# Modulation's matrix-vector product moved from the first FFN to the branch merge, and waits per tile in place of four barriers

## The chip, the cores and the metric

The kernel runs on one core of one Trainium2 chip. The metric is the time of one execution on the device in microseconds (us), the median of three runs. A core has TensorE (PE, matmuls), VectorE (DVE), ScalarE (ACT), GpSimd (POOL) and SyncE (SP), which here only issues DMAs. Each engine runs its own instructions in order and waits on semaphores for the others.

## The reference

The program is three transformer blocks one after the other on 512 tokens of width 1024, all in float32. The two places that matter here are the merge of the first block's two branches, and the modulation of the third block, which depends on nothing but two inputs:

```python
# first block
g_a, g_b = jnp.split(gates, 2, axis=-1)
mixed = jax.nn.sigmoid(g_a) * ya + jax.nn.sigmoid(g_b) * yb
x = x + mixed @ w_out[l]
h = rmsnorm(x, norm_ffn_g[l])
u = causal_dwconv(h @ w_up[l], ffn_conv_w[l], ffn_conv_b[l])
val, gt = jnp.split(u, 2, axis=-1)
x = x + (jax.nn.gelu(gt) * val) @ w_down[l]
...
# third block
mod = (jax.nn.silu(c) @ w_ada[l] + b_ada[l]).reshape(b_, N_SUB, 3, D_MODEL)
shift, scale, gate = mod[:, :, 0], mod[:, :, 1], mod[:, :, 2]
```

w_ada is 1024 x 9216, c one row of 1024: a matrix-vector product that reads 36 MB. ya and yb are the outputs of the two branches, each a product of its own.

## The kernel before

Activations lie feature-major: tiles k = 0 to 7 of 128 features by 512 tokens. X is the residual; HH and HL are the high and low parts of the normalised input, YH and YL those of another operand. Every matmul of float32 precision is three matmuls of reduced precision (`exact3`, L312): high by high, high by low, low by high. A tile of 128 output features over 8 k is 24 matmuls.

Weights come in 189 panels of 128 x 2048 (1 MB), two tiles of the usual kind each, through two slots. For each panel SP issues the DMA into WT (`panel`, L223), ACT casts it into WH (`next_panel`, or `hi` in the FFN loops), POOL subtracts into WL (`low`, L275), and PE opens it (`open_panel`) once POOL is done. SP may load a panel when POOL has finished the one two before it (w_lo), ACT may cast it when PE has opened the one before (w_used). G_MERGE, G_OUT1 and G_FFN1 are panels 15, 27 and 31.

The order is written out by hand in blocks of code, one per engine. Around the change it is: the diff attention branch (da); the merge, four times two gate panels and one branch panel, in which ACT takes sigmoids of the gates into GS and DVE multiplies and adds into MIX; OUT1, four panels, with DVE adding the result to X (`add_out`, L1650); FFN1, eleven chunks of two up panels and one down panel; a small embedding stage, stick-breaking attention (SB), OUT2, latent attention (MLA), OUT3, FFN2, the third block's mixer with OUT4, and FFN3. `end_phase` is a barrier of PE, ACT and DVE: each drains, counts up phase_end and waits for the two others.

The first tiles of an FFN are "raw": PE works on the input before it is normalised, and DVE scales the result in the accumulator (by NRS, L1891), while `normalise` makes HH and HL for the others.

The modulation is 36 slabs of w_ada (1 MB each, three buffers ADA), in halves: DVE multiplies a half-slab by the row CROW, silu(c) (`ada`, L1868), ACT sums it over its 1024 columns into a column of MOD (`sums`, L1226). SP issues them in FFN1's loop, three panels then three slabs a chunk (L259); a slab waits for the sums of the slab three before (ada_used).

## Time and profile before

| | |
|---|---|
| median of 3 runs | 2812.05 us (2810.21 to 2819.77) |
| profiled execution | 2812.49 us, span 2810.7 us, TensorE's mean granted clock 0.945 |
| busy share of the span | PE 89%, PE weight load 71%, DVE 49%, ACT 36%, POOL 37% |
| merge, 367.7 to 500.4 | 132.7 us, PE 132.65 busy |
| OUT1, 510.7 to 556.5 | 45.8 us, PE 45.78 busy |
| DMA | 245.49 MB, mean 87 GB/s |

A row of a timeline has the start, the length, the engine with the line of the kernel, the operation with its output and inputs, and in brackets how long the engine sat idle before it and who released it. Matmuls overlap: their spacing from start to start is shorter than their length. The clock of TensorE is given as a share of full speed (2.4 GHz); 0.5 is its lower level. A q behind an engine's name (SPq, DVEq) means its instruction queue. The landing of a DMA is counted from its issue.

### The profile page before, as it was taken

To read this page: it belongs to the slowest core of one execution; us is meant where nothing else is said; L and a number is where in the kernel's file an instruction comes from. 1 tells how busy PE (TensorE), PEld (TensorE's weight loads), DVE (VectorE), ACT (ScalarE), POOL (GpSimd) and SP (SyncE) were. 2 spreads that over 40 slices of the span, in tenths; PEclk is the share of its full clock that TensorE was granted. 3 is DMA by queue.
4 is the path that set the end of the run, shared out by engine and by line. 5 is a ranking of instruction groups with operands and counts; after the bars stand their busy time and mean duration, and the time that the engine had idled before them with its cause. 6 is when DMAs were issued, how large, how long until landed. Compare 5 with 4: busy or idle time off the path is not lost.

```text
span 2810.7 us, 31316 instructions
## 1 busy us (share of the span) xinstructions
PE 2515.1 (89%) x11582; PEld 1998.7 (71%) x11582; DVE 1377.8 (49%) x1881; ACT 1018.1 (36%) x1294; POOL 1034.5 (37%) x758
## 2 busy tenths in 40 slices
PE   7968889879999789998898889999979998899996
PEld 5636668657777668776776677888858766588885
DVE  6373621478888865244444554232265343622225
ACT  4322422333334453466436533122234332322211
POOL 3202134435555344222343234445434203254442
PEclk9878999989999999999898999999989998899998
DMA  3102012324444322111122112222312101122221
GB/s 139 50 30 75 31 60 105 135 105 179 179 182 189 152 76 90 61 45 46 60 90 75 46 53 83 91 103 90 104 60 85 69 17 60 45 90 104 90 101 48
DMA packets 35811, 245.49 MB, mean 87 GB/s; under 512 B 3935, under 2 KB 3935, under 8 KB 7044
## 3 DMA queue, kind: packets, MB, share of 16 engines
q1 hardware_dynamic: 34704, 241.73, 23.8%
q10 hardware_dynamic: 1012, 2.45, 0.3%
q8 instruction: 65, 1.06, 0.1%
q14 instruction: 30, 0.25, 0.0%
HBM read 242.06 MB, written 2.11 MB: 87 GB/s over the span
## 4 chain that ended last, share of the span: by engine, by line
issue 57%; POOL 27%; PE 13%; DVE 2%; DVEq 0%; POOLq 0%; ACT 0%; ACTq 0%
POOL WL L279 27%; PE PS L314 4%; PE PS L315 4%; PE PS L316 4%; DVE X L2186 0%; DVE ARENA L2181 0%; DVE ARENA L1591 0%; DVE ARENA L1609 0%; POOLq L283 0%; DVEq L2185 0%; DVE ARENA L1616 0%; DVE ARENA L2313 0%; DVEq L1632 0%; PE PS L372 0%; POOLq L276 0%
## 5 line engine op out<-in xcount | busy, mean ns | idle before, releaser
L279 POOL TENSOR_TENSOR WL<-WT,WH 128x512 fp32r<-128x512 f32 x754 | 1034.3, 1403 | 1734.6 <-ACT WH L960 1225.9
L314 PE MATMUL PS<-HH,WH 128*128 128x512 f32 x1520 | 609.6, 401 | 47.4 <-DVE HL L1623 12.8
L316 PE MATMUL PS<-HH,WL 128*128 128x512 f32 x1520 | 599.9, 395 | 0.0
L315 PE MATMUL PS<-HL,WH 128*128 128x512 f32 x1520 | 599.6, 395 | 0.0
L314 PE MATMUL PS<-YH,WH 128*128 128x512 f32 x904 | 363.6, 402 | 59.2 <-ACT ARENA L954 18.9
L314 PEld LDWEIGHTS PS<-HH,WH 128*128 128x128 f32 x1520 | 290.5, 191 | 126.9 <-issue 26.5
L1238 ACT CAST WH<-WT 128x2048 fp32r<-128x2048 f32 x90 | 172.1, 1912 | 559.9 <-PE PS L314 559.9
L315 PE MATMUL PS<-YL,WH 128*128 128x512 f32 x904 | 358.3, 396 | 0.0
L316 PE MATMUL PS<-YH,WL 128*128 128x512 f32 x904 | 358.0, 396 | 0.0
L316 PEld LDWEIGHTS PS<-HH,WL 128*128 128x128 f32 x1520 | 290.0, 191 | 62.4
L315 PEld LDWEIGHTS PS<-HL,WH 128*128 128x128 f32 x1520 | 290.8, 191 | 58.0 <-issue 0.9
L960 ACT CAST WH<-WT 128x2048 fp32r<-128x2048 f32 (+1 forms) x99 | 187.4, 1893 | 199.3 <-PE PS L314 156.9
L954 ACT ACTIVATE ARENA<-PS 128x512 f32<-128x512 f32 (+1 forms) x162 | 111.5, 693 | 396.6 <-PE PS L316 286.9
L314 PEld LDWEIGHTS PS<-YH,WH 128*128 128x128 f32 x904 | 173.0, 191 | 108.6 <-ACT ARENA L954 20.0
L954 ACT ACTIVATE ARENA<-ARENA 128x512 f32<-128x512 f32 (+6 forms) x195 | 167.4, 878 | 165.8 <-DVE ARENA L1763 44.4
L1905 DVE TENSOR_TENSOR ARENA<-PS,ARENA 128x512 f32<-128x512 f32 x44 | 30.4, 692 | 376.6 <-PE PS L316 376.6
L316 PEld LDWEIGHTS PS<-YH,WL 128*128 128x128 f32 x904 | 173.5, 192 | 37.6
L315 PEld LDWEIGHTS PS<-YL,WH 128*128 128x128 f32 x904 | 173.8, 192 | 34.7
L1927 DVE TENSOR_TENSOR ARENA<-PS,ARENA 128x512 f32<-128x512 f32 x176 | 121.7, 691 | 114.9 <-PE PS L316 113.4
L389 PE MATMUL PS<-HH,WH 128*128 128x512 f32 x256 | 110.4, 431 | 41.2 <-DVE HL L1603 19.9
L954 ACT ACTIVATE ARENA<-PS,COLS 128x128 f32<-128x128 f32 (+3 forms) x102 | 57.7, 567 | 190.4 <-DVE COLS L2264 72.5
L314 PE MATMUL PS<-WH,HH 128*128 128x256 f32 x384 | 112.3, 292 | 14.5 <-DVEq L1573 7.2
(285 smaller groups left out, 3387.2 us busy)
## 6 DMA issues: line engine op xcount, KB each, us to landing
WT<-weights SPq DMA_DIRECT2D x188, 1024.0 KB, 4.8
ARENA<-w_ada SPq DMA_DIRECT2D x36, 1024.0 KB, 6.7
X<-x_fm SPq DMA_DIRECT2D x4, 512.0 KB, 8.0
out_fm<-X SPq DMA_DIRECT2D x8, 256.0 KB, 2.0
ARENA<-rel_rows ACTq DMA_DIRECT2D x1, 1024.0 KB, 5.2
CON<-constants SPq DMA_DIRECT2D x1, 704.0 KB, 10.1
WT<-weights SPq DMA_DIRECT2D x1, 512.0 KB, 5.4
ARENA<-rows SPq DMA_DIRECT2D x1, 512.0 KB, 5.8
```

The costliest lines, as they stand in the source:

```text
L279: i = nc.gpsimd.tensor_tensor(WL[s][:, e], WT[s][:, e], WH[s][:, e].bitcast(F32), ALU.subtract)
L314: i0 = nc.tensor.matmul(o, w[0], r[0], start=first, stop=False, skip_group_check=True)
L315: nc.tensor.matmul(o, w[0], r[1], start=False, stop=False, skip_group_check=True)
L316: i2 = nc.tensor.matmul(o, w[1], r[0], start=False, stop=last, skip_group_check=True)
L389: i0 = nc.tensor.matmul(psb(b), w[0], src[0][:, k, :], start=k == 0, stop=False, skip_group_check=True)
L954: return nc.scalar.activation(o, i, fn, **kw)
L960: nc.scalar.copy(WH[s][:, 0:width], WT[s][:, 0:width]).then_inc(sem("w_hi"), 1)
L1238: nc.scalar.copy(WH[s][:, :], WT[s][:, :]).then_inc(sem("w_hi"), 1)
L1905: free(tt(GT[:, q, :], psb(b), GE[:, q, :], ALU.mult), b)
L1927: tt(dst[:, j, :], psb(4 + j % 4), dst[:, j, :], ALU.add).then_inc(sem("b_read"), 1)
```

## The change

The modulation's 72 half-slabs move from FFN1 to the merge (60) and OUT1 (12). The row silu(c) lies in accumulator banks 4 and 5 (CROWP) instead of in SBUF. The four barriers after the diff attention, after the merge, before OUT2 and before OUT3 go; the branch panels wait for da_done, and an output GEMM's first tile waits for each of its eight input tiles (mix_ready, sy_ready, mly_ready). MIX is split into HH and HL tile by tile in DVE's last merge step. The raw input of FFN1 goes to YH and YL, so that four tiles of chunk 0 can be raw. In all FFNs the last chunk's product is made during the down GEMM of the chunk before it (`early`), the last two chunks standing outside the loop. Three norm sums add their last square on PE instead of DVE (`two_parts`), and PE waits for the constants at the first norm sum instead of before the first tile.

```diff
         a = Carve()
         CV, GE, GT = a.tiles(4), a.tiles(2), a.tiles(2)
         ada_at = a.at
+        a = Carve(ada_at + 3 * 2048)
+        PIN = a.tiles(2)
+        a = Carve(14 * S)
         ADA = [a(2048) for _ in range(3)]
-        PIN = a.tiles(2)
         CROW = a(D)
+        CROWP = PSF[:, 4 * S:4 * S + D]
         ACC = ARENA[:, ada_at:ada_at + DT * S].rearrange("p (k n) -> p k n", k=DT)
 
         a = Carve()
...
-            stream(2, G_FFN1 + 2)
-            sp.wait_ge(sem("phase_end"), 3 * 3)
+            stream(2, G_MERGE + 2)
+            sp.wait_ge(sem("da_done"), 1)
             sp.dma_start(CROW, rows_in[:, 1536:1536 + D]).then_inc(sem("c_dma"), 16)
-            sp.dma_start(PIN, p_in).then_inc(sem("p_dma"), 16)
             for k in range(3):
                 ada(k, k, first=True)
-
-            with sp.Fori(0, (CH - 1) // 2) as i:
-                for h in range(2):
-                    g = G_FFN1 + 2 + 6 * i + 3 * h
-                    for k in range(3):
-                        panel(g + k, (G_FFN1 + 3 * h + k) % 2)
-                    for k in range(3):
-                        ada(3 + 6 * i + 3 * h + k, k)
-            panel(G_FFN1 + 3 * CH - 1, (G_FFN1 + 3 * CH - 1) % 2)
+            for i in range(12):
+                panel(G_MERGE + 2 + i, (G_MERGE + 2 + i) % 2)
+                for k in range(3 if i < 10 else 0):
+                    ada(3 + 3 * i + k, k)
+            stream(G_MERGE + 14, G_FFN1)
             for k in range(3):
-                ada(NADA - 3 + k, k)
-            stream(G_PLE, n_panels)
+                ada(33 + k, k)
+            stream(G_FFN1, G_FFN1 + 2)
+            sp.wait_ge(sem("ada_used"), NADA)
+            sp.dma_start(PIN, p_in).then_inc(sem("p_dma"), 16)
+            stream(G_FFN1 + 2, n_panels)
             store()
 
 
...
-            def out_gemm(g0):
+            def out_gemm(g0, src, ready):
                 for g in range(g0, g0 + 4):
                     open_panel(g)
-                    feature_tiles(g, g % 2, 8, 256, y_hi, y_lo, (0, P))
+                    for c in (0, P):
+                        b = take()
+                        for k in range(DT):
+                            if g == g0 and c == 0:
+                                pe.wait_ge(sem(ready), k + 1)
+                            i0, i2 = exact3(psb(b), wtile(g % 2, 8, 256, k, c, c + P), (src[0][:, k, :], src[1][:, k, :]), k == 0, k == DT - 1)
+                            if c == 0 and k == 0:
+                                used(g, i0)
+                        i2.then_inc(sem("a_done"), 1)
...
-            end_phase()
 
 
             for jp in range(4):
                 for q in range(2):
                     panel_h(G_MERGE + 3 * jp + q)
                 g = open_panel(G_MERGE + 3 * jp + 2)
+                pe.wait_ge(sem("da_done"), 1)
                 ym = lambda k, o=0: YH[:, k + o, :]
                 for j in range(2):
                     for br in range(2):
                         feature_tiles(g, g % 2, 4, 256, lambda k: YH[:, 4 * br + k, :], lambda k: YL[:, 4 * br + k, :],
                                       (P * j,), base=1024 * br, first_of_panel=(j == 0 and br == 0))
-            pe.wait_ge(sem("mix_ready"), 1)
-            end_phase()
-            out_gemm(G_OUT1)
-
-
-            def ffn(g0, sums="one", shift=None):
+            out_gemm(G_OUT1, (HH, HL), "mix_ready")
...
-                        if raw and q < 2:
-                            raw_tile(g, P * q, b, opens=q == 0, sums=None if q else sums, last=q == 1,
+                        if raw and q < raws:
+                            raw_tile(g, P * (q % 2), b, src, opens=q % 2 == 0, sums=None if q else sums, last=src[0] is HH and q == raws - 1,
                                      shift=None if shift is None else (shift, SHIFT_BANKS[q]))
-                            if q:
+                            if q == raws - 1:
...
-                            i0, i2 = exact3(psb(b), wtile(s, 2, D, k, P * j, P * j + P), (YH[:, k, :], YL[:, k, :]), k == 0, k == 1)
+                            i0, i2 = exact3(psb(b), wtile(s, 2, D, k, P * j, P * j + P), (YH[:, 4 * last + k, :], YL[:, 4 * last + k, :]), k == 0, k == 1)
...
-            end_phase()
-
+
+
+            ada_at = [0]
+
+            def ada_sums(count):
+                for j in range(ada_at[0], ada_at[0] + count):
+                    w = ADA[j // 2 % 3][:, D * (j % 2):D * (j % 2) + D]
+                    act.wait_ge(sem("ada_mul"), j + 1)
+                    i = f(w, w, ACT.Copy, accum_out=MOD[:, j:j + 1])
+                    if j % 2:
+                        i.then_inc(sem("ada_used"), 1)
+                ada_at[0] += count
 
             for jp in range(4):
                 for q in range(2):
-                    gate_panel(G_MERGE + 3 * jp + q, [GS[:, 2 * q, :], GS[:, 2 * q + 1, :]], ACT.Sigmoid)
-                act.drain().then_inc(sem("gs_ready"), 1)
+                    next_panel(G_MERGE + 3 * jp + q)
+                    for e in range(2):
+                        b = take()
+                        i = f(GS[:, 2 * q + e, :], psb(b), ACT.Sigmoid)
+                        free(i, b)
+                        if q and e:
+                            act.drain().then_inc(sem("gs_ready"), 1)
+                        if jp or q:
+                            ada_sums(3)
+                    if jp == 0 and q == 0:
+                        act.wait_ge(sem("c_dma"), 16)
+                        f(CROWP, CROW, ACT.Silu).then_inc(sem("c_ready"), 1)
                 next_panel(G_MERGE + 3 * jp + 2)
                 skip(4)
+                if jp < 3:
+                    ada_sums(6)
                 act.wait_ge(sem("gs_used"), jp + 1)
-            end_phase()
-            out_gemm(G_OUT1, lambda k: par("norm_ffn", k))
+            for q in range(4):
+                next_panel(G_OUT1 + q)
+                skip(2)
+                if q:
+                    for k in (2 * q - 2, 2 * q - 1):
+                        raw(lambda k: par("norm_ffn", k), k, k + 1, YH)
+                        ada_sums(2)
+            sqrt_ahead()
+            raw(lambda k: par("norm_ffn", k), 6, DT, YH)
+            settle()
...
-                normalise(shift, last=t0 + 1, meanwhile=open_third)
                 if conv:
+                    high(g0 + 2, g0 % 2)
+                    normalise(shift)
                     mid(0)
-                    sums(0, range(4))
+                else:
+                    normalise(shift, last=t0 + 1, meanwhile=open_third)
...
-            end_phase()
-
+            dve.drain().then_inc(sem("da_done"), 1)
+
+
+            ada_at = [0]
+
+            def ada(count):
+                for j in range(ada_at[0], ada_at[0] + count):
+                    s, e = j // 2 % 3, j % 2
+                    if e == 0:
+                        dve.wait_ge(sem(f"ada_dma{s}"), 16 * (j // 6) + 16)
+                    w = ADA[s][:, D * e:D * e + D]
+                    tt(w, w, CROWP, ALU.mult).then_inc(sem("ada_mul"), 1)
+                ada_at[0] += count
+
+            def mix_split(k):
+                nc.vector.tensor_copy(HH[:, k, :], MIX[:, k, :])
+                dve.drain()
+                tt(HL[:, k, :], MIX[:, k, :], HH[:, k, :].bitcast(F32), ALU.subtract).then_inc(sem("mix_ready"), 1)
 
             for jp in range(4):
                 skip(4)
+                if jp == 0:
+                    dve.wait_ge(sem("c_ready"), 1)
+                ada(12 if jp else 6)
                 dve.wait_ge(sem("gs_ready"), jp + 1)
                 for j in range(2):
                     dst = MIX[:, 2 * jp + j, :]
+                    if jp == 3:
+                        mix_split(3 * j)
                     b = take()
                     free(tt(dst, psb(b), GS[:, 2 * j, :], ALU.mult), b)
+                    ada(2 if jp < 3 else 0)
+                    if jp == 3:
+                        mix_split(3 * j + 1)
+                        mix_split(3 * j + 2)
                     b = take()
                     free(tt(MT[:, j, :], psb(b), GS[:, 2 * j + 1, :], ALU.mult), b)
-                dve.drain().then_inc(sem("gs_used"), 1)
-                for j in range(2):
-                    tt(MIX[:, 2 * jp + j, :], MIX[:, 2 * jp + j, :], MT[:, j, :], ALU.add)
-                dve.drain()
-            for k in range(8):
-                nc.vector.tensor_copy(YH[:, k, :], MIX[:, k, :])
-            dve.drain()
-            for k in range(8):
-                i = tt(YL[:, k, :], MIX[:, k, :], YH[:, k, :].bitcast(F32), ALU.subtract)
-            i.then_inc(sem("mix_ready"), 1)
-            end_phase()
-            add_out(lambda k: par("norm_ffn", k))
+                    ada(1 if jp < 3 else 0)
+                    if jp == 3:
+                        dve.drain()
+                        tt(dst, dst, MT[:, j, :], ALU.add)
+                if jp < 3:
+                    dve.drain().then_inc(sem("gs_used"), 1)
+                    for j in range(2):
+                        tt(MIX[:, 2 * jp + j, :], MIX[:, 2 * jp + j, :], MT[:, j, :], ALU.add)
+                    dve.drain()
+            dve.drain().then_inc(sem("gs_used"), 1)
+            mix_split(6)
+            mix_split(7)
+
+            def ada_out(k):
+                if k < 6:
+                    ada(2)
+
+            add_out(lambda k: par("norm_ffn", k), (YH, YL), ada_out)
...
+                        if early and j == 1:
+                            gated(CH - 1)
+                        if early and j == 2:
+                            gated_hi(4)
+                        if early and j == 4:
+                            gated_lo(4)
```

SP's order. WT0 and WT1 are the two slots of the weight panels, ARENA<-w_ada a slab, ARENA<-rows the row c. Before, the slabs begin in FFN1, after the wait for the third barrier (phase_end); row 14 is in the loop over all earlier panels, row 21 a panel of FFN1's chunks:

```order
13 L235 COMPARE_AND_BRANCH
14 L225 DMA WT0<-weights 128x2048 [waits w_lo]
15 L254 DMA ARENA<-rows 128x1024 [waits phase_end]
16 L255 DMA ARENA<-p_fm 128x1024
17 L250 DMA ARENA<-w_ada 128x2048 x3
18 L259 UNCONDITIONAL_BRANCH
19 L259 ISA
20 L225 ISA [waits w_lo]
21 L225 DMA WT1<-weights 128x2048
```

After, with the merge's panels from the third on in rows 17, 19 and 21:

```order
14 L228 DMA WT0<-weights 128x2048 [waits w_lo]
15 L257 DMA ARENA<-rows 128x1024 [waits da_done]
16 L253 DMA ARENA<-w_ada 128x2048 x3
17 L228 DMA WT1<-weights 128x2048 [waits w_lo]
18 L253 DMA ARENA<-w_ada 128x2048 [waits ada_used] x3
19 L228 DMA WT0<-weights 128x2048 [waits w_lo]
20 L253 DMA ARENA<-w_ada 128x2048 [waits ada_used] x3
21 L228 DMA WT1<-weights 128x2048 [waits w_lo]
```

Each of the panels G_MERGE + 2 to G_MERGE + 12 now stands behind three slabs, and but for the first three slabs each of these waits for sums of ACT.

ACT in the merge, before (CAST WH is the cast of the next panel, ACTIVATE ARENA<-PS a sigmoid):

```order
176 L954 ACTIVATE ARENA<-PS 128x512 [waits a_done] x2
177 L960 CAST WH0<-WT0 128x2048 [waits w_used,w_dma0]
178 L954 ACTIVATE ARENA<-PS 128x512 [waits a_done] x2
179 L960 CAST WH1<-WT1 128x2048 [waits w_used,w_dma1]
180 L960 CAST WH0<-WT0 128x2048 [waits w_used,w_dma0,gs_used]
```

After (ACTIVATE ARENA,MOD<-ARENA is the sum of a half-slab):

```order
182 L967 CAST WH1<-WT1 128x2048 [waits w_used,w_dma1,gs_used]
183 L961 ACTIVATE ARENA<-PS 128x512 [waits a_done]
184 L961 ACTIVATE ARENA,MOD<-ARENA 128x1024 [waits ada_mul] x3
185 L961 ACTIVATE ARENA<-PS 128x512 [waits a_done]
186 L961 ACTIVATE ARENA,MOD<-ARENA 128x1024 [waits ada_mul] x3
187 L967 CAST WH0<-WT0 128x2048 [waits w_used,w_dma0]
```

Six sums stand between the casts of two panels.

ACT at FFN1's opening, before: the Silu of c, the cast of FFN1's second panel, the root of the norm, and the tiles HH of the normalised input with the third panel's cast among them:

```order
213 L954 ACTIVATE ARENA<-ARENA 128x1024 [waits c_dma]
214 L960 CAST WH0<-WT0 128x2048 [waits w_used,w_dma0]
215 L954 ACT_TABLE_LOAD
216 L954 ACTIVATE ARENA<-PS,PAR 128x512 [waits ms_ready]
217 L1038 CAST HH<-ARENA 128x512 [waits raw_used,nt_ready] x6
218 L960 CAST WH1<-WT1 128x2048 [waits w_used,w_dma1]
```

After:

```order
245 L967 CAST WH0<-WT0 128x2048 [waits w_used,w_dma0]
246 L961 ACTIVATE ARENA<-PS,PAR 128x512 [waits ms_ready]
247 L967 CAST WH1<-WT1 128x2048 [waits w_used,w_dma1]
248 L1044 CAST HH<-ARENA 128x512 [waits nt_ready] x8
249 L961 ACT_TABLE_LOAD
```

The Silu of c is gone from here, and the cast of the third panel stands ahead of the tiles of HH.

## Rows read from the trace of the kernel before

**Rows 1.** Page, part 1: busy time, share of the span and instructions of each engine.
```profile
PE 2515.1 (89%) x11582; PEld 1998.7 (71%) x11582; DVE 1377.8 (49%) x1881; ACT 1018.1 (36%) x1294; POOL 1034.5 (37%) x758
```

**Rows 2.** Windows: length, then busy (instructions) by engine, clock, DMA share, GB/s.
```profile
367.70:500.40 132.70, 132.65 (x576) 109.37 (x576) 14.26 (x21) 33.34 (x29) 60.43 (x48) 0.98 0.26 91
...
612.90:923.20 310.30, 299.96 (x1296) 243.36 (x1297) 258.31 (x287) 118.41 (x153) 170.09 (x108) 0.99 0.48 184
923.20:988.00 64.80, 49.07 (x192) 38.22 (x192) 47.65 (x63) 32.20 (x48) 23.57 (x16) 0.89 0.29 109
...
1780.10:1812.70 32.60, 32.60 (x145) 27.01 (x144) 8.96 (x14) 6.83 (x5) 15.63 (x13) 1.00 0.27 97
```

**Rows 3.** PE's timeline, after waits: start, length, operation, idle time and releaser.
```profile
367.75 0.79 PE L314 MATMUL PS<-HH,WH 128*128 128x512 f32 x1 [6.37 <-DVEq L1573]
...
510.72 0.77 PE L314 MATMUL PS<-YH,WH 128*128 128x512 f32 x1 [10.27 <-PEq L297]
...
575.42 0.76 PE L314 MATMUL PS<-HH,WH 128*128 128x512 f32 x1 [7.11 <-DVE HL L1623]
...
612.88 0.80 PE L314 MATMUL PS<-HH,WH 128*128 128x512 f32 x1 [4.53 <-POOL WL L279]
...
649.25 0.47 PE L314 MATMUL PS<-HH,WH 128*128 128x512 f32 x1 [1.15 <-DVE ARENA L1665]
...
683.52 0.47 PE L314 MATMUL PS<-HH,WH 128*128 128x512 f32 x1 [1.15 <-DVE ARENA L1665]
...
950.77 0.77 PE L314 MATMUL PS<-YH,WH 128*128 128x512 f32 x1 [5.37 <-issue]
...
1651.07 0.47 PE L314 MATMUL PS<-YH,WH 128*128 128x512 f32 x1 [2.27 <-PEq L297]
...
2060.54 0.47 PE L314 MATMUL PS<-YH,WH 128*128 128x512 f32 x1 [3.05 <-issue]
...
2775.99 0.47 PE L314 MATMUL PS<-YH,WH 128*128 128x512 f32 x1 [3.05 <-issue]
```

**Rows 4.** DMA: page part 6; SP's and ACT's timeline at 948; one panel; one window.
```profile
WT<-weights SPq DMA_DIRECT2D x188, 1024.0 KB, 4.8
...
948.47 0.33 SPq L250 DMA_DIRECT2D ARENA<-w_ada  x1
949.18 0.34 SPq L225 DMA_DIRECT2D WT<-weights  x1
...
DMA to landing us min/median/max: 7.3/7.3/7.3
...
956.48 1.91 ACT L960 CAST WH<-WT 128x2048 fp32r<-128x2048 f32 x1 [8.04 <-DMA WT<-weights]
...
672.00:680.00 8.00, 8.00 (x37) 6.63 (x36) 7.85 (x7) 3.76 (x5) 5.92 (x4) 1.00 1.01 425
```

**Rows 5.** Groups by line, window 640 to 920: DVE's product of a half-slab.
```profile
L1873 DVE TENSOR_TENSOR ARENA<-ARENA 128x1024 f32<-128x1024 f32 x48 | 63.4, 1321 | 2.3
```

**Rows 6.** ACT's timeline: a sigmoid, a wait for a product, a sum, a cast.
```profile
380.81 0.60 ACT L954 ACTIVATE ARENA<-PS 128x512 f32<-128x512 f32 x1 [4.84 <-PE PS L316]
...
603.70 1.05 ACT L954 ACTIVATE ARENA<-ARENA 128x1024 f32<-128x1024 f32 x1
...
604.74 1.90 ACT L1238 CAST WH<-WT 128x2048 fp32r<-128x2048 f32 x1
...
947.30 1.06 ACT L954 ACTIVATE ARENA<-ARENA 128x1024 f32<-128x1024 f32 x1 [3.60 <-DVE ARENA L1873]
```

**Rows 7.** POOL's timeline: the four subtractions of a panel, in FFN1 and FFN2.
```profile
606.72 6.11 POOL L279 TENSOR_TENSOR WL<-WT,WH 128x512 fp32r<-128x512 f32 x4 [18.62 <-ACT WH L1238]
...
1787.75 5.05 POOL L279 TENSOR_TENSOR WL<-WT,WH 128x512 fp32r<-128x512 f32 x4 [5.59 <-ACT WH L1238]
```

**Rows 8.** PE's timeline: two matmuls in a row, 3 us after a wait.
```profile
2063.46 0.63 PE L316 MATMUL PS<-YH,WL 128*128 128x512 f32 x1
2063.89 0.63 PE L314 MATMUL PS<-YH,WH 128*128 128x512 f32 x1
```

More of the change, by code:

```diff
@@ L1224, in mid @@
                             free(f(GE[:, q, :], psb(b), ACT.Silu), b)
-                def sums(step, js):
-                    for j in js if conv else ():
-                        w = ADA[j // 2][:, D * (j % 2):D * (j % 2) + D]
-                        act.wait_ge(sem("ada_mul"), 6 * step + j + 1)
-                        i = f(w, w, ACT.Copy, accum_out=MOD[:, bass.ds(6 * step + j, 1)])
-                        if j % 2:
-                            i.then_inc(sem("ada_used"), 1)
                 def hi(k, gk):
@@ L1247, in open_third @@
                 def open_third():
-                    if not conv:
-                        gate(1)
+                    gate(1)
                     high(g0 + 2, g0 % 2)
@@ L1272, in ffn @@
                             mid(c + 1)
-                            sums(c + 1, range(4))
-                sums(CH - 1, (4, 5))
                 next_panel(g0 + 3 * CH - 1)
                 if conv:
-                    sums(CH, (0, 1))
                     raw(lambda k: par("norm_ple", k))
@@ L1285, in ffn @@
                     n["cv"] = v0 + 2 * CH
-                return sums
-            act.wait_ge(sem("c_dma"), 16)
-            f(CROW, CROW, ACT.Silu).then_inc(sem("c_ready"), 1)
-            ada_sums = ffn(G_FFN1, True)
+            ffn(G_FFN1, True)
             for j in range(8):
@@ L1954, in ffn @@
                         product(c + 1)
+                up(CH - 2)
+                down(CH - 3)
+                product(CH - 2)
                 if conv_on:
@@ L1962, in ffn @@
                     i.then_inc(sem("p_ready"), 1)
+                up(CH - 1)
+                down(CH - 2, early=True)
                 down(CH - 1, last=True)
@@ L1965, in ffn @@
                 trail(DT - 1, (lambda k: par("norm_ple", k)) if conv_on else None)
-                if conv_on:
-                    for j in range(2, 6):
-                        ada(NADA // 3 - 1, j)
                 tiles[0] = t0 + 4 * CH
@@ L2168, in _ @@
             n["att"] = NQ * MLA_HEADS
-            end_phase()
+            dve.drain()
             nc.vector.memset(ACC[:, :, :], 0.0)
```

104 lines of the change are left out of this document (46 added, 58 removed).

## The prediction

> **What bounds the kernel now.** I read the busy times first: PE works 2515.1 of 2810.7 us [rows 1], so it is the engine to keep fed, and what the change is worth is what it does to PE's idle time. Second, the stretches around the change [rows 2]: in the merge PE is full (132.65 of 132.70 us), POOL is 46% busy, ACT 25%, DVE 11%, and the DMA share is 0.26. In FFN1's ten middle chunks (612.9 to 923.2) PE has 299.96 of 310.30 us, DVE 258.31. Third, PE's own rows where it had waited [rows 3]: 6.37 us before the merge, 10.27 before OUT1, 7.11 and 4.53 in FFN1's opening, 1.15 in each later chunk, 5.37 before FFN1's last product, 3.05 at the same place in FFN2 and FFN3.
>
> Two lengths of the same work tell what the modulation costs today: a chunk without it takes 32.6 us, all of it PE (144 matmuls at 0.227) [rows 2]; FFN1's come 34.25 apart, each with its wait of 1.15 [rows 3]. So modulation stretches FFN1 through DVE and ACT. The merge looks like the better host: engines with 75% and more of idle time.
>
> **But the merge is a different loop.** Its panel (1 MB) lasts 10.88 us on PE (48 matmuls of 0.227), and the new code gives each panel a slot of six half-slabs: 3 MB more, six DVE products, six ACT sums. Each resource alone fits in 10.88: 4 MB at 425 GB/s [rows 4] is 9.9 us, six products of 1.32 are 7.9 [rows 5], a cast, two sigmoids and six sums at their pitch of 1.04 us [rows 6] are 1.85 + 1.0 + 6.24 = 9.1. The order of the queues makes a ring of them. SP issues slab, slab, slab, then the panel; each slab waits for the sums of the slab three back (ada_used), so the panel for slot p+1 can't be asked for until ACT has ended the last sum of slot p. It then queues behind up to three slabs in the DMA queue, and ACT's next instruction is that panel's cast. Nothing overlaps the chain sums, issue, landing, cast.
>
> **Price of one slot.** Call S the end of the slot's last sum. The third slab goes at S + 0.2, the panel at S + 0.5 or 0.6 (an issue takes 0.33 [rows 4]). A lone 1 MB lands 4.8 us after its issue in the median, and a panel issued 0.71 us after a slab lands after 7.3 [rows 4]: 2.5 us, or 1 MB at 425 GB/s, per transfer in front, 2.3 us of latency. Slabs one and two went at about S - 4.3 and S - 1.9, so the engines are busy from about S - 2 on: four transfers end at S + 0.3, 2.9, 5.3 and 7.8. The panel is there at S + 7.8. Cast 1.85, then sigmoids and sums 7.24: a gate slot lasts 16.9 to 17.1, a branch slot (no sigmoids) 16.3 to 16.5. PE is given a panel each 17 us and needs 10.88 plus 2 of slow clock after a wait (below), so it idles 4 to 5 us a slot. DVE's products wait for slabs that are there before the panel, and stay beside the chain. PE doesn't stand in the way: it opens panel p some 5.3 us after that panel's cast, ends it 16 to 18 us after it, and the slot's second sigmoid comes at 20.6.
>
> **The merge as a whole.** First slot: the row and the first slabs wait for da_done at about +6.3 (the end of the 6.37 wait); row, three slabs and the panel behind them land at +20.1, the cast ends at +22.0 (all from 361.4). Then seven gate slots of 17.05 and three branch slots of 16.4 make 168.6: the cast of OUT1's first panel ends at +190.6. POOL's four subtractions take 5 to 7 (5.04 alone, 6.11 beside DVE [rows 7]; I take 7, DVE being full): OUT1 opens at 361.4 + 197.6 = 559.0, against 510.7 now. **+48.3**, and that already contains what the removed barriers give: the 6.37 and 10.27 us are gone, covered by waits that are longer. If the panel landed as a lone one does, 4.8 after its issue, a slot would be 14.5 and the loss 23; if ring and DVE products joined in series (one product, 1.3, per slot) it would be 61.
>
> The Trainium skill, page "SBUF — State Buffer", section "Summary: rules for kernel authors", says to reckon HBM-to-SBUF time at about 358 GB/s. The trace differs: 425 over 8 us [rows 4]. By the page 1 MB would take 2.93 instead of 2.46 us, the panel of each slot would land 1.7 later, and the estimate for the merge would be 17 more.
>
> **FFN1 without modulation.** DVE loses 72 products, ACT 72 sums, SP the slabs between panels.
> - Opening: two products of 1.22 us no longer stand in DVE's chain to the first normalised tile, four tiles instead of two work on unnormalised input while DVE normalises (PE's 7.11 wait [rows 3] shrinks, though the matmuls after it are the same), the cast at 604.74 no longer stands behind four sums (4 x 1.04 = 4.1) [rows 6], and POOL's row of 6.11 comes nearer to the 5.04 of an undisturbed panel [rows 7]. The Silu of c leaves the way to the root, but OUT1's last accumulation comes some 3 later, since ACT and DVE carry twelve half-slabs there: these two I set against each other. Together 7.4, and the 4.53 wait before 612.88 goes with the slow clock behind it: 9.8.
> - Chunks: (34.25 - 32.65) x 8 = 12.8.
> - Last product during the down before: 5.37 goes, of which 3.9 remains a gain after DVE's slower additions.
> - End: the cast at 956.48, which waited 8.04 for a panel behind a slab [rows 4], is free: 4.9. Root and last sums: 0.9.
> Sum **-32.3**. Its bounds: at least 26 (chunks, end and product, half the opening), at most 38 (a DVE with 72 products less slows POOL less).
>
> **The other joints.** SB to OUT2 and MLA to OUT3: the barrier before an output GEMM becomes a wait per tile, 2.27 in the trace [rows 3] plus a little drain: 2.4 each. FFN2's last product (3.05, and about 2.2 of slow clock behind it: its matmuls run at a pitch of 0.43 at first [rows 8], where a full chunk has 0.227): 5.2. FFN3's: 3.2. Sum **-13.2**, bounds 9 and 16. The summing in two parts and the moved wait for constants cost and give nothing: squares of ACT end last there.
>
> **Clock.** In the stretches with waits the granted clock is 0.89 [rows 2], and after a wait of 3 us or more some nine matmuls run at 1.2 GHz [rows 8], about 2 us lost. In the merge this lies inside the slot, since PE waits for the ring.
>
> **Sum.** +48.3 - 32.3 - 13.2 = +2.8 us on the profiled execution's 2812.49, which is 0.4 above the median of the runs shown (2812.05). I forecast **2815**.
>
> **Rivals.**
> (A) The ring doesn't hold: panels come as soon as now, PE stays full in the merge. Then the merge gains the barriers' 6.4 and 10.3 less some 7 (panel three, behind the row and the first slabs, is late in any case) instead of losing 48: 2812.5 - 9.7 - 45.5 is about 2757. For it: every resource alone fits in 10.88 us [rows 4 to 6]. Against: SP is one queue in order, and its order, shown above, has the panel behind three waits. Chance 0.10.
> (B) Slower: the ring is longer than reckoned. ACT's sum waits for a DVE product which starts only when the third slab has landed, and DVE still has another product or a gating row in hand: from about 0.8 us a slot on (8 over ten slots) this decides; one product, 1.3 to 1.5, gives +13 to +15: 2829. For it: in FFN1 a sum waited 3.60 us for its product [rows 6]. Against: slabs land 2.5 us before the panel. Chance 0.19.
> (B2) Slower too: the transfers of this loop come 0.4 us further apart than the 2.5 of [rows 4]. Four a slot are 1.7, over ten slots 17: 2832. Against: 425 GB/s held over 8 us, in which slabs and panels alternated as here. Chance 0.06. It is what the rate on the page "SBUF — State Buffer" of the Trainium skill would do.
> (C) The ring is shorter: DMA takes the slabs up so early that only one stands in front of the panel, 2.5 a slot less over ten slots, -25; or half of that, with FFN1 giving 36: 2790 to 2807, say 2800. Chance 0.20.
> (D) As forecast, 2807 to 2823: 0.45.
>
> **How the numbers follow.** A and a good half of C leave by more than 0.3% to the fast side (0.3%, or 8.4 us, is about what a measurement of this kernel can tell from no change): 0.10 + 0.13 = 0.23. Both B lie beyond 2820.5 for the most part, with a tail of D: 0.22 + 0.07 = 0.29. The rest, 0.48, is no change. The range takes C and most of B: 2795 to 2835; A and the far ends, 0.17, are left out.
>
> **What would show it.** PE full in the merge stretch would refute the ring; right is a PE share near 70% there, a wait of 4 to 5 us before each of panels three to twelve put down to POOL's subtraction, ACT's cast waiting about 7 to 8 us for the DMA, and the merge lasting 190 to 200 us. FFN1's chunk period should be 32.6. No wait should be left before OUT2, OUT3 and the last down of FFN2. I am wrong if slabs land so early that ACT never waits, or if FFN1's opening keeps its waits.

## The result, and the profile after

The changed kernel takes 2839.19 us (median of 4 runs, 2834.82 to 2840.91) against 2812.39 (median of four runs of the kernel before): a ratio of 1.0086, 95% interval 1.0071 to 1.0102. It is slower by 26.8 us. The prediction had 2815 with a range up to 2835, and called no change the likeliest outcome. The profiled execution has a span of 2836.9 us against 2810.7.

Page, part 1, of the changed kernel, against [rows 1]:

```profile
PE 2533.7 (89%) x11588; PEld 2014.3 (71%) x11588; DVE 1381.6 (49%) x1880; ACT 1016.9 (36%) x1294; POOL 1010.8 (36%) x758
```

PE is busy 18.6 us longer with almost the same matmuls (six more, of the norm sums in two parts), so part of the loss is slow clock. The stretches of the changed kernel, against [rows 2] (columns: window, length, busy time and instructions of PE, PEld, DVE, ACT, POOL, clock, DMA share, GB/s): the merge's start beside the end of the attention branch, the rest of its first two panels with the wait for the third, the ten panels that stand behind slabs, OUT1, FFN1.

```profile
361.40:370.20 8.80, 8.80 (x34) 7.08 (x33) 8.03 (x4) 4.26 (x4) 5.65 (x4) 0.82 0.00 0
370.20:391.90 21.70, 14.33 (x64) 11.53 (x62) 7.08 (x7) 9.83 (x13) 4.93 (x4) 0.92 0.55 220
391.90:575.70 183.80, 131.17 (x480) 103.64 (x480) 94.61 (x94) 85.04 (x137) 53.25 (x40) 0.84 0.62 234
575.70:621.40 45.70, 45.64 (x193) 37.66 (x194) 29.44 (x30) 27.34 (x40) 22.51 (x17) 0.96 0.43 161
621.40:1008.40 387.00, 369.04 (x1598) 302.04 (x1597) 264.99 (x332) 96.66 (x89) 180.23 (x132) 0.98 0.26 94
```

The third row holds the answer: 480 matmuls that need 109 us at full clock take 183.8, and no engine is full there (PE 71%, DVE 51%, ACT 46%, POOL 29%) nor is the DMA (0.62). A stretch in which nothing is full is bound by a chain. PE's timeline shows the same place from its side; four of its eleven waits, the last of them at the opening of OUT1:

```profile
391.91 0.80 PE L315 MATMUL PS<-YH,WH 128*128 128x512 f32 x1 [7.38 <-POOL WL L280]
412.83 0.79 PE L315 MATMUL PS<-HH,WH 128*128 128x512 f32 x1 [8.14 <-POOL WL L280]
429.48 0.79 PE L315 MATMUL PS<-HH,WH 128*128 128x512 f32 x1 [4.10 <-POOL WL L280]
...
575.76 0.79 PE L315 MATMUL PS<-HH,WH 128*128 128x512 f32 x1 [7.25 <-POOL WL L280]
```

POOL is only the messenger: its subtraction starts when ACT's cast has ended, and ACT's timeline says what that waited for.

```profile
411.87 1.04 ACT L961 ACTIVATE ARENA<-ARENA 128x1024 f32<-128x1024 f32 x1
412.82 0.19 ACT L961 ACTIVATION_READ_ACCUMULATOR ARENA<-ARENA 128x1 f32 x1
422.47 1.91 ACT L967 CAST WH<-WT 128x2048 fp32r<-128x2048 f32 x1 [9.47 <-DMA WT<-weights]
```

The slot's last sum ends at 412.9, SP issues the third slab at once and the panel 0.37 later, and the cast stands 9.47 us until the panel lands. ACT's waits over the merge, in total, times and longest (window 391 to 575), and the landing of the panels issued there (window 390 to 560):

```profile
ACT WH L967 <- DMA WT<-weights: 92.0, 10, 10.6
...
DMA to landing us min/median/max: 8.0/8.9/11.0
```

92.0 us of waiting for panels in ten slots; in the kernel before a panel of the merge landed 4.8 us after its issue and nobody waited.

Where the 26.2 us between the spans come from, by the offset of the second trace against the first at the same instruction:

| stretch | before | after | change | forecast |
|---|---|---|---|---|
| start to OUT1's opening | 510.72 | 575.76 | +65.0 | +48.3 |
| to the embedding stage's opening | 975.92 | 1008.47 | -32.5 | -31.4 |
| to stick-breaking's last stretch | 1341.94 | 1374.81 | +0.3 | -0.9 |
| OUT2 | 1476.28 | 1504.41 | -4.7 | -2.4 |
| MLA and OUT3 | 1717.93 | 1744.52 | -1.5 | -2.4 |
| FFN2 and the norm behind it | 2125.72 | 2148.53 | -3.8 | -5.2 |
| third block's mixer | 2353.13 | 2382.37 | +6.4 | 0 |
| OUT4 | 2428.41 | 2456.96 | -0.7 | 0 |
| FFN3 and the end | 2810.7 | 2836.9 | -2.3 | -3.2 |

### The profile page after: what moved, and what is told of

Read it like the earlier page. It is cut to its first block, busy times and chain, and to the rows that moved or that the text cites. A ratio compares the mean times of both kernels' runs of the same rounds, so it can differ in the third digit from the quotient of the medians.

```text
span 2836.9 us, 31001 instructions
## 1 busy us (share of the span) xinstructions
PE 2533.7 (89%) x11588; PEld 2014.3 (71%) x11588; DVE 1381.6 (49%) x1880; ACT 1016.9 (36%) x1294; POOL 1010.8 (36%) x758
## 4 chain that ended last, share of the span: by engine, by line
issue 58%; POOL 26%; PE 13%; DVE 2%; DVEq 1%; POOLq 0%; ACT 0%; ACTq 0%
POOL WL L280 26%; PE PS L315 4%; PE PS L316 4%; PE PS L317 4%; DVE X L2238 0%; DVE ARENA L2233 0%; DVE ARENA L1610 0%; POOLq L284 0%; DVEq L2237 0%; DVE ARENA L1628 0%; DVEq L1919 0%; DVE ARENA L1635 0%; DVEq L1651 0%; PE PS L377 0%; POOLq L277 0%
## 5 line engine op out<-in xcount | busy, mean ns | idle before, releaser
L280 POOL TENSOR_TENSOR WL<-WT,WH 128x512 fp32r<-128x512 f32 x754 | 1010.6, 1371 | 1787.2 <-ACT WH L967 1268.5
L315 PE MATMUL PS<-HH,WH 128*128 128x512 f32 x1568 | 631.5, 403 | 64.2 <-POOL WL L280 41.2
L316 PE MATMUL PS<-HL,WH 128*128 128x512 f32 x1568 | 621.7, 396 | 0.0
L317 PE MATMUL PS<-HH,WL 128*128 128x512 f32 x1568 | 621.3, 396 | 0.0
L315 PE MATMUL PS<-YH,WH 128*128 128x512 f32 x840 | 336.5, 401 | 47.5 <-POOL WL L280 23.2
L316 PE MATMUL PS<-YL,WH 128*128 128x512 f32 x840 | 332.3, 396 | 0.0
L317 PE MATMUL PS<-YH,WL 128*128 128x512 f32 x840 | 331.8, 395 | 0.0
L961 ACT ACTIVATE ARENA<-ARENA 128x512 f32<-128x512 f32 (+7 forms) x194 | 167.1, 875 | 147.0 <-DVE ARENA L1785 44.3
L317 PEld LDWEIGHTS PS<-YH,WL 128*128 128x128 f32 x840 | 160.9, 192 | 34.3
L316 PEld LDWEIGHTS PS<-YL,WH 128*128 128x128 f32 x840 | 161.1, 192 | 32.5
L395 PE MATMUL PS<-HH,WH 128*128 128x512 f32 x240 | 104.8, 437 | 37.2 <-DVE HL L1622 32.5
```

Of the source, the lines that this page charges most:

```text
L280: i = nc.gpsimd.tensor_tensor(WL[s][:, e], WT[s][:, e], WH[s][:, e].bitcast(F32), ALU.subtract)
L315: i0 = nc.tensor.matmul(o, w[0], r[0], start=first, stop=False, skip_group_check=True)
L316: nc.tensor.matmul(o, w[0], r[1], start=False, stop=False, skip_group_check=True)
L317: i2 = nc.tensor.matmul(o, w[1], r[0], start=False, stop=last, skip_group_check=True)
L395: i0 = nc.tensor.matmul(psb(b), w[0], src[0][:, k, :], start=k == 0, stop=False, skip_group_check=True)
L961: return nc.scalar.activation(o, i, fn, **kw)
```

## The experiments

**The panel a batch ahead.** If the ring is the cause, the order of one queue decides everything:

```diff
-            stream(2, G_MERGE + 2)
+            stream(2, G_MERGE + 3)
...
-            for i in range(12):
-                panel(G_MERGE + 2 + i, (G_MERGE + 2 + i) % 2)
+            for i in range(11):
+                panel(G_MERGE + 3 + i, (G_MERGE + 3 + i) % 2)
                 for k in range(3 if i < 10 else 0):
                     ada(3 + 3 * i + k, k)
```

> The changed kernel with one difference: in SP's queue each panel of the merge stands one batch of three slabs earlier, so that its DMA no longer waits for the sums of its slot. Ring theory: in the changed kernel a slot of the merge lasts 18.1 us on average (PE's openings at 391.91 to 575.76 us, ten slots), of which the cast's wait for the panel is 8.3 to 9.5. With the panel ahead that wait goes; what is left is the slabs' own ring (issue 0.3, landing 4.9 to 7, product 2.3, sums 2.1 for three slabs, at least 9.5 to 12) or PE's 10.88. Slots of 11 to 13 us, merge 50 to 70 us shorter, the kernel at 2770 to 2790 us. Rival, DMA bandwidth: 4 MB a slot take what they take whatever the order; then slots stay near 18 and the time near 2839. Rival, ACT or DVE is the bound: slots stay at 15 or more, since their work is the same.

2759.15 us (4 runs), ratio to the kernel before 0.9805, interval 0.9788 to 0.9822. 80 us less than the changed kernel, 2% under the one before, by the order of the same instructions in SP's queue. The slots are as expected (11.4 us), the time is 11 us below the expected range: OUT1 opens 78.6 us earlier, not 50 to 70. The merge from just ahead of the first slabs (issued at 369) to OUT1's opening at 497.13, and OUT1, in windows of this kernel:

```profile
367.00:497.10 130.10, 126.38 (x550) 102.30 (x548) 92.59 (x92) 97.01 (x150) 57.96 (x45) 1.00 0.94 358
497.10:542.00 44.90, 44.26 (x193) 36.01 (x194) 34.07 (x39) 27.13 (x39) 22.71 (x16) 1.00 0.46 167
```

PE 97% busy at full clock, ACT 75%, DVE 71%, and now it is the DMA that is nearly full: 0.94, 358 GB/s. A panel's landing is no shorter than before (median 9.5), but it is no longer waited for. PE's waits in all of the merge (window 362 to 500), and ACT's costliest group of waits (window 391 to 575):

```profile
PE PS L315 <- POOL WL L280: 2.8, 3, 1.4
PE PS L315 <- DVE ARENA L1894: 0.7, 1, 0.7
...
ACT ARENA L961 <- DVE ARENA L1869: 15.2, 18, 2.6
```

Engine work and bytes are those of the changed kernel, so both rivals of this run (bandwidth, DVE or ACT as the bound) fall.

**A smaller dose.** The same, but with the panel issued between the second and the third slab:

```diff
-                panel(G_MERGE + 2 + i, (G_MERGE + 2 + i) % 2)
                 for k in range(3 if i < 10 else 0):
                     ada(3 + 3 * i + k, k)
+                    if k == 1:
+                        panel(G_MERGE + 3 + i, (G_MERGE + 3 + i) % 2)
```

> The changed kernel with each panel of the merge issued after the second slab of the batch before it instead of after the third of its own: it no longer waits for the last third of the sums, and has one slab less in front of it. A dose between the changed kernel and the one with the panel a whole batch ahead. Ring theory: the panel's issue comes 2 us or more earlier and its landing takes 7 instead of 8.8 us: slots of 12 to 15 us, kernel at 2775 to 2810 us. Bandwidth or engine bound: near 2839.

2794.11 us, ratio 0.9923, interval 0.9906 to 0.9940. It lies between, and the slots follow the wait: 15.1 us, at the edge of what I expected. ACT's casts waited 57.5 us for panels in the ten slots (window 386 to 530), against 92.0 and none; the second row is the wait of one more cast, which the profile puts down to no releaser:

```profile
ACT WH L970 <- DMA WT<-weights: 51.6, 9, 7.2
ACT WH L970 <- issue: 5.9, 1, 5.9
```

**Transfers alone.** Products and sums left out, and a slab that waits for the landing of the slab three back:

```diff
-                    sp.wait_ge(sem("ada_used"), aidx - 2)
+                    sp.wait_ge(sem(f"ada_dma{s}"), 16 * (aidx // 3))
...
-                    act.wait_ge(sem("ada_mul"), j + 1)
-                    i = f(w, w, ACT.Copy, accum_out=MOD[:, j:j + 1])
+                    i = f(MOD[:, j:j + 1], par("eps"), ACT.Copy)
...
-                    if e == 0:
-                        dve.wait_ge(sem(f"ada_dma{s}"), 16 * (j // 6) + 16)
-                    w = ADA[s][:, D * e:D * e + D]
-                    tt(w, w, CROWP, ALU.mult).then_inc(sem("ada_mul"), 1)
```

> The changed kernel without the modulation's products and sums (it leaves out the matrix-vector product; a column each is filled instead): the slabs are still loaded in the same order ahead of the panels, but a slab waits for the landing of the slab three back, not for sums. Ring theory: the panel is asked for as soon as its slot is free and four transfers have gone out; with 4 MB in 10.88 us the DMA share of the merge comes to 0.9 or more, and PE is nearly full: slots of 10.9 to 12.5 us, kernel at 2765 to 2785 us. If the four transfers by themselves hold the panel back (a bandwidth of less than 385 GB/s in this mix, or a latency per wait), slots are 13 us or more.

2763.77 us in one run, slots of 10.8. Eight of them in one window of this kernel:

```profile
392.00:478.00 86.00, 86.00 (x373) 71.09 (x374) 12.18 (x18) 24.63 (x62) 40.26 (x32) 0.98 1.01 425
```

PE has no idle time at a DMA share of 1.01 and 425 GB/s, with all three slabs still ahead of the panel. So slabs ahead of a panel do no harm in themselves; what does is that they wait for sums. (This run takes the products and sums off DVE and ACT as well; that their work isn't what held the merge is shown by the panel a batch ahead, which keeps it.) Both the slots and the time are just below what I expected. The 425 bears on the rate weighed in the prediction, from the page "SBUF — State Buffer" of the Trainium skill (section "Summary: rules for kernel authors", 358 GB/s for HBM-to-SBUF): the trace doesn't agree, since on this lone core 425 holds over 86 us.

The four kernels side by side. A slot is the spacing of ACT's casts of panels G_MERGE + 2 to G_OUT1, mean of ten:

| kernel | slot | ACT's wait for panels | OUT1 opens | time |
|---|---|---|---|---|
| changed | 18.3 | 92.0 | 575.76 | 2839.19 |
| panel before the third slab | 15.1 | 57.5 | 534.75 | 2794.11 |
| panel a batch ahead | 11.4 | none | 497.13 | 2759.15 |
| transfers alone | 10.8 | 4.7 | 504.60 | 2763.77 |

**The norm sums in one part.**

```diff
-            norm_sum(two_parts=True)
+            norm_sum()
```

(three times, with DVE's `trail` and ACT's `settle` as in the kernel before.)

> The changed kernel with the three norm sums in one part again (DVE adds the last square). The prediction gave the two parts 0. The trace of the changed kernel shows the root after FFN2 coming 4.1 us after the last square where it came 2.1 after it before, with a second pair of matmuls of 1.9 us at half the clock. If the second part costs: 2 to 5 us less than 2839, that is 2834 to 2837. If it is the clock alone that moved: the same 2839.

2833.26 us, ratio to the kernel before 1.0070, interval 1.0049 to 1.0092; 5.9 less than the changed kernel, though the intervals of the two ratios overlap. It looks like the second part's price, and the sections don't bear that out. By the spacing of ACT's casts, the stretch around the norm after FFN2 became 1.3 us shorter, the one around OUT4's 2.1 longer and the end 0.3 shorter: together nothing, as forecast. Most of the 5.9 lies ahead of OUT1's opening (1.7) and in the attention of the third block (109.9 us instead of 114.2), both places with unchanged code. What does happen at the norm after FFN2 can be read in the changed kernel (PE, then ACT):

```profile
2096.45 2.05 PE L374 MATMUL PS<-ARENA,CON 128*128 128x512 f32 x2 [3.34 <-DVE ARENA L1628]
2098.29 1.91 PE L377 MATMUL PS<-ARENA,CON 128*128 128x512 f32 x2
...
2095.56 0.63 ACT L961 ACTIVATE ARENA<-ARENA 128x512 f32<-128x512 f32 x1 [0.80 <-DVEq L1651]
...
2100.24 0.69 ACT L961 ACTIVATE ARENA<-PS,PAR 128x512 f32<-128x512 f32 x1 [2.76 <-PE PS L377]
```

Two sums one behind the other at half the clock take 3.7 us; the second pair takes the place of a DVE addition of 0.7.

**Both.** The panel a batch ahead and the sums in one part:

```diff
-            stream(2, G_MERGE + 2)
+            stream(2, G_MERGE + 3)
...
-            norm_sum(two_parts=True)
+            norm_sum()
```

> The kernel with the panel a batch ahead (2759.15 us) and, added, the three norm sums in one part again, which alone took 2839 to 2833. If the two are independent, as the theory says (the one is in the merge, the other after FFN2, OUT4 and FFN3): 2752 to 2757 us. If the gain of the one part was a shift of the clock in the attention of the third block, it may be absent here: 2759.

2758.98 us, ratio 0.9810, interval 0.9782 to 0.9838: the same as with two parts, and not the 2752 to 2757 of two independent gains. So no gain of one part is shown; of the 6 us seen above, 4.3 were a shorter spell of slow clock in the attention.

**The joints alone**, in the kernel before:

```diff
-            pe.wait_ge(sem("sy_ready"), SB_PAIRS)
-            end_phase()
-            out_gemm(G_OUT2)
+            out_gemm2(G_OUT2, (YH, YL), "sy_ready")
...
-            pe.wait_ge(sem("mly_ready"), MLA_HEADS)
-            end_phase()
-            out_gemm(G_OUT3)
+            out_gemm2(G_OUT3, (YH, YL), "mly_ready")
```

> The kernel before with one part of the change alone: the barriers ahead of OUT2 and OUT3 replaced by waits per tile. The prediction gave 2.4 us each, 4.8 together. The trace of the changed kernel shows 4.7 at OUT2 and 3.5 at OUT3 (offsets of the two traces against each other). By the prediction 0.9983 of the time before, by the trace 0.997. If a wait per tile only takes the barrier's place, 1.000.

2814.16 us (10 runs), ratio 1.0006, interval 0.9990 to 1.0022: no difference. Its trace is 8.9 us ahead of the kernel before from FFN2 on, and 9.3 are lost again in the third block's attention, 116.0 us instead of 106.7. Of the 8.9, 2.9 were there before the first place that was edited; 3.9 come at OUT2 and 2.0 from there to FFN2. Even these aren't all the edit's: the kernel with the early product alone, below, which has the old barriers, comes 1.6 us further ahead at OUT2 too.

**The late product**, in the changed kernel:

```diff
-                down(CH - 2, early=True)
+                down(CH - 2)
+                product(CH - 1)
                 down(CH - 1, last=True)
```

> The changed kernel with the last chunk's product of each FFN made after the down before it again. The prediction gave the early product 3.9 (FFN1) + 5.2 (FFN2) + 3.2 (FFN3) = 12.3 us: 2851 us. If DVE's extra work inside the down gives part of it back, 2843 to 2848; if it is hidden anyway, 2839.

2844.13 us, ratio 1.0126, interval 1.0096 to 1.0156: 4.9 more. Section by section the early product is worth nearly what was forecast: between the same casts of both kernels FFN1 is 5.6 us longer without it, FFN2 2.0, FFN3 4.0, together 11.6 against 12.3, though spread otherwise. The total moved less because in this run OUT1 opened 6 us earlier (slots of 17.8) and the stretch from FFN1's last cast to FFN2's start was 3.8 shorter, both with unchanged code. The wait that came back before FFN1's last down:

```profile
988.52 0.77 PE L315 MATMUL PS<-YH,WH 128*128 128x512 f32 x1 [4.23 <-issue]
```

**A mere shift.** Each of these kernels lost 3 to 9 us against the kernel before in an attention stage whose code is the same. So I delayed the kernel before, by reciprocals on tiles that nobody reads any more, and changed nothing else:

```diff
             i.then_inc(sem("mix_ready"), 1)
+            for k in range(1):
+                nc.vector.reciprocal(MIX[:, k, :], MIX[:, k, :])
             end_phase()
```

> The kernel before with one DVE reciprocal of 128 x 512 (3.35 us in its trace) on a tile nobody reads any more, ahead of the barrier before OUT1: nothing else changes, all that follows comes 3.4 us later. Question: why did the joints alone, 8.9 us ahead of the kernel before after OUT3, end 1.9 behind it? In their profile the third block's attention (panels 152 to 156) takes 116.0 us instead of 106.7, with TensorE at 1.2 GHz for about 40 us instead of 26. Theory C: how long the clock stays low there depends on the history of the run, so that any shift can move it: here the attention takes 110 to 116 us and the kernel is 3.4 + 3 to 9 slower. Theory D: the long spell is brought about by the changed joints and norms themselves: the attention stays at 107 and the kernel is 3.4 slower.

The same with `range(3)`:

> The same with three reciprocals, 10.1 us. Theory C: the attention's length differs from 106.7 by some us in one of the two at least, either way. Theory D: 106.7 again, the kernel 10.1 slower.

2817.01 us (ratio 1.0027, interval 1.0016 to 1.0038) and 2820.85 (1.0039, 1.0025 to 1.0053). The attention of the third block, from the same cast to the same cast, in the kernel before, the two shifted ones and the changed one:

```profile
2268.80:2375.50 106.70, 100.41 (x411) 68.23 (x410) 37.49 (x83) 32.47 (x68) 20.98 (x16) 0.87 0.10 35
2272.50:2382.40 109.90, 102.64 (x411) 68.84 (x410) 36.69 (x83) 32.46 (x69) 20.99 (x16) 0.86 0.10 34
2274.80:2389.10 114.30, 107.08 (x411) 70.67 (x410) 37.55 (x83) 32.52 (x67) 21.00 (x16) 0.82 0.10 33
2290.50:2404.70 114.20, 106.97 (x410) 70.74 (x409) 37.55 (x83) 32.55 (x68) 20.98 (x16) 0.82 0.09 32
```

The same matmuls (410 or 411 records), nearly the same work on DVE, ACT and POOL; what differs is the clock, 0.87, 0.86 and 0.82. Theory D, as it stands, falls: the attention of the changed kernel, to within 0.1 us, appears in the kernel before with none of the changed joints and norms. That the delay brought it about, theory C, isn't shown. The rival is that the spell differs from one execution to the next of the same kernel, and each kernel has one profile. The medians speak for caution: 10.1 us of delay cost 11.0 (interval 7.0 to 14.9), which is D's number, and the profiled execution of that kernel (2826.86) is the slowest of its five; 3.4 us of delay cost 7.6 (4.5 to 10.7). So a +6.4 there needs none of the changed code, but how much of it belongs to the changed kernel's median stays open.

**The early product alone**, in the kernel before, for FFN2 and FFN3:

```diff
+                        if early and j == 1:
+                            gated()
+                        if early and j == 2:
+                            gated_hi(4)
+                        if early and j == 4:
+                            gated_lo(4)
...
+                    up(CH - 1)
+                    down(CH - 2, early=True)
```

> The kernel before with one part of the change alone: the last chunk's product made during the down before it, in FFN2 and FFN3. Up to the end of FFN2 the prediction gave 5.2 us, at FFN3 3.2. From the traces: 5 by the last panel of FFN2 and 3.3 at FFN3's, together 8.3 if the attention between them keeps its 106.7 us; 0 to 5 if it takes 110 to 116 us, as in every changed kernel so far.

2806.56 us (10 runs), ratio 0.9984, interval 0.9970 to 0.9998. Its trace has FFN2 3.0 us and FFN3 3.3 us shorter, with the attention at 109.9. The profiled execution is the fastest of the ten (2797.05), and most of its lead isn't the edit's: it is 12.3 us ahead of the kernel before when FFN2 begins, in stages with the same code. The two waits of 3.05 in [rows 3] are what is gained. The extra 2.2 that I had added at FFN2 for slow clock behind its wait is not there.

## Why the prediction was wrong

**The mechanism was right.** SP's order made a ring of sums, issue, landing and cast; PE was held by it once per panel, though every engine and the DMA had room; ACT waited for the DMA, and the wait goes in steps as the panel is taken out of the ring. The merge's row refutes rival A (PE full in the merge): PE 71% there, near the 70% that the prediction named as its sign. The kernel with the panel a batch ahead, where PE is full, runs at 2759, about the 2757 that A reckoned for a full PE. No wait of PE is left before OUT2, OUT3 and the last down of FFN2, as forecast.

**The step that failed is the price of one slot.** I had 16.9 to 17.1 for a gate slot and 16.4 for a branch slot, 168.6 for ten; measured are 18.3 on average, 182.6: 14.0 of the 16.7 by which the merge was missed. Within the slot it is one term, the landing. I let four transfers follow each other 2.5 us apart from S - 2 on, so that the panel landed at S + 7.8, and ACT would have waited 78 us in ten slots; it waited 92.0, the 14.0 that are missing. From its issue the panel took 8.9 us in the median, not 7.3. The transfers of one slot (issued at 408.9, 411.0, 413.0 and 413.4):

```profile
DMA to landing us min/median/max: 4.8/4.8/4.8
...
DMA to landing us min/median/max: 6.1/6.1/6.1
...
DMA to landing us min/median/max: 6.9/6.9/6.9
...
DMA to landing us min/median/max: 9.0/9.0/9.0
```

They land at 413.7, 417.1, 419.9 and 422.4: gaps of 3.4, 2.8 and 2.5, and over the ten slots 3.0, 3.2 and 2.7 in the mean. The rate of [rows 4] holds for a queue that is kept full, as in the transfers alone; here, behind an almost empty queue, the first transfers come further apart. The row that I had taken the 2.5 from says the same when it is read rightly: I subtracted the landing time of a lone transfer from that of the panel (7.3 - 4.8), but the panel was issued 0.71 later than its slab. The slab of 948.47 landed after 4.9, at 953.4, the panel at 956.5: a gap of 3.1. With 3.1 for each of the three gaps the panel would land at S + 9.6, against the 9.2 that ACT waited on average. The size of this term is itself not fixed: the merge is the same code in the kernels with the norm sums in one part and with the late product, and their ten slots took 179.6 and 177.8 us, so the price was short by 9 to 14.

The remaining 2.7 lie at the start, 3.4 late, less 0.7 saved at POOL. DVE's last steps of the attention branch now run beside POOL's first panel of the merge, which the barrier had kept apart. DVE's timeline of the kernel before, then of the changed one:

```profile
365.60 0.75 DVE L1786 SCALAR_TENSOR_TENSOR ARENA<-ARENA,PAR 128x512 f32<-128x512 f32 x1
366.42 0.43 DVE L1635 CAST YH<-ARENA 128x512 fp32r<-128x512 f32 x1
366.92 0.69 DVE L1637 TENSOR_TENSOR YL<-ARENA,YH 128x512 fp32r<-128x512 f32 x1
```


```profile
365.37 1.72 DVE L1808 SCALAR_TENSOR_TENSOR ARENA<-ARENA,PAR 128x512 f32<-128x512 f32 x1
367.17 1.36 DVE L1654 CAST YH<-ARENA 128x512 fp32r<-128x512 f32 x1
368.60 1.62 DVE L1656 TENSOR_TENSOR YL<-ARENA,YH 128x512 fp32r<-128x512 f32 x1
```

So da_done, and with it the row and the first slabs, came 2.6 us later than reckoned. I had let the row go at the end of the old wait; what the barrier covered, DVE and POOL not working at the same time, I had not priced.

**FFN1.** -32.5 up to the embedding stage against -31.4: right in size. No wait of PE over 0.3 us is left between 672 and the last chunk at 965.94 (2.02 there), so the chunks run at PE's pace. The opening gave 9.7 against 9.8 (from OUT1's opening to the matmul behind the second wait, 102.16 us before and 92.50 after), but not as reckoned: of its two waits one hardly shrank (6.26 against 7.11), which I had named as a sign of being wrong, and the other is 1.91 instead of 4.53 and not gone. That the sum came out is partly luck. The early product was worth more there (5.6 against 3.9).

**The other joints.** OUT2 gave 4.7, twice the forecast, not all of it the joint's by the experiment above; MLA and OUT3 1.5 against 2.4; FFN2 less by the clock term, as its own experiment shows (the prediction's slow clock after every wait of 3 us or more doesn't hold everywhere: behind FFN3's wait of 3.05 the granted clock of the kernel before stays at 1.00); FFN3 3.3 against 3.2 in the kernel with the early product alone, 2.3 in the changed one. Their sum of -13.2 came out as -12.3 in the changed kernel's table (4.7, 1.5, 3.8, 2.3), inside its bounds, by errors that cancel.

**The clock.** I gave the third block's mixer 0, since nothing in it changes. In the profiled executions it cost 6.4, by a longer spell at 1.2 GHz. This is the second error of the working: a range for a sum of ten terms needs one for the stages without a term. With 14.0 at the ring, 2.7 at its start and 6.4 here, 23 of the 24 us between 2815 and 2839 are named.

**The rivals.** The first B came out in size (13 to 15 a merge) and not in mechanism: ACT waited for the DMA in all ten slots, never for a product. B2 came out in both: the transfers of this loop come further apart than 2.5 us, 1.4 us in sum over the three gaps of a slot, where it had 1.7 for four, and 14 us over the merge, where it had 17. What it isn't is a lower rate of a full queue, which was 425 GB/s. Its chance of 0.06 was too low, since the landing was priced from a single row.

## What to carry to other kernels

A transfer that stands behind waiting transfers in an in-order queue inherits their waits: read the new order of the issuing queue first, and price the loop that it closes, sums, issue, landing, cast, before the capacity of any engine. Where such a ring shows, move the critical transfer ahead of the waiting ones; here one batch was worth 80 us, and turned a loss of 0.9% into a gain of 2%. A gain of a few microseconds must be looked for in its own section of the trace, since the total can hide it or invent it; and even there, compare with what unchanged sections move by.

## What the runs showed of the hardware

TensorE's clock in a stage with the same code is not a constant. In the third block's attention, of small matmuls, the granted clock fell to 1.2 GHz in every kernel, but not at the same place: 38 us after the stage's first cast in the kernel before and in three others (the norm sums in one part, the shift by 3 us, the early product alone), and 30 us after it in the eight that are left. In the first group it stayed low for 24 to 27 us, in the second for 41; some had a second, much shorter spell later. That made the stage 106.7 or 109.9 us long in the first group and 114.2 to 116.0 in the second. Two windows each show it, of the kernel before and of the one shifted by 10 us: the 30 us ahead are alike (29.69 and 29.63 us busy at full clock), and in the next 10 the one has 0.91, the other 0.50:

```profile
2268.80:2298.80 30.00, 29.69 (x143) 19.49 (x141) 10.23 (x31) 11.08 (x28) 5.03 (x4) 1.00 0.10 36
2298.80:2308.80 10.00, 9.69 (x45) 5.80 (x45) 4.90 (x16) 3.63 (x11) 0.00 (x0) 0.91 0.01 2
...
2274.80:2304.80 30.00, 29.63 (x143) 19.43 (x141) 10.29 (x31) 11.02 (x27) 5.04 (x4) 1.00 0.10 36
2304.80:2314.80 10.00, 9.75 (x30) 6.14 (x31) 2.79 (x10) 1.77 (x6) 0.00 (x0) 0.50 0.00 0
```

What decides between an early and a late fall, and so between a long and a short spell, stays open: one profile a kernel can't tell it, and the kernel before itself spreads from 2802.7 to 2819.8 us over its runs. It bounds what can be claimed of single small edits here: for the joints the sections say 5.9 us and the total 0, for the norm sums the sections say 0 and the total 6.

DVE slowed beside POOL, by a factor of 2.3 to 3.2 in the three pairs of rows above, of operations with their operands in SBUF. The modulation's products show where that ends. With the row in SBUF a product took 1.21 us at the least and up to 2.20 (the kernel before; those that ran wholly beside POOL 1.41 in the median, those without it 1.22). With the row in an accumulator bank all 72 took 1.21 to 1.22, also the 30 that ran wholly beside POOL in the kernel with the panel a batch ahead. That kernel first, then the kernel before (durations in ns, least, median and most):

```profile
L1869 DVE TENSOR_TENSOR ARENA<-ARENA,PS x72: 1206/1214/1223, 374.9 to 539.8; 128x1024 f32<-128x1024 f32 x72
...
L1873 DVE TENSOR_TENSOR ARENA<-ARENA x69: 1208/1220/2195, 600.1 to 980.3; 128x1024 f32<-128x1024 f32 x69
```
